# Eight scatter results over six PSUM banks: chunks 0, 1 and 4 in the banks of the up product and of the first result half

## The chip, the cores and the metric

One NeuronCore of a Trainium2 chip runs the whole program. The metric is the device time of one execution in microseconds; a kernel's time is the median of its runs. The trace comes from one profiled execution.

## The reference, cut to what matters

A decoder trunk of two layers over 512 tokens of width 1024, all float32. Each layer adds a mixer (a convolution block in layer 0, gated linear attention in layer 1), a cross-attention over 256 memory tokens, and a mixture of 32 experts of which each token uses 2. The change lies in the mixture of experts alone:

```python
def expert_block(args):
    xb, e = args
    return (jax.nn.silu(xb @ w_gate[e]) * (xb @ w_up[e])) @ w_down[e]

y_buf = lax.map(expert_block, (x_buf.reshape(n_blocks, MOE_BLOCK, D), block_expert)).reshape(-1, D)
y = y_buf[dest] * g_flat[order][:, None].astype(h.dtype)
out = jnp.zeros((T, D), h.dtype).at[token_idx].add(y)
```

Every expert has a 1024x512 gate matrix, a 1024x512 up matrix and a 512x1024 down matrix. Each expert's result rows are weighted and added to the rows of the tokens that chose it.

## The kernel before

**Tiling.** The residual stream xT is kept transposed: 8 chunks of 128 channels by 512 tokens. The experts are taken in 16 pairs per layer (`NP`), two experts with up to 64 tokens each side by side in the 128 columns of TensorE. A second, branched loop (`ROUNDS`) serves inputs where an expert has more than 64 tokens; it isn't entered with these inputs. Weights stream from HBM through a ring of six 2 MB slots, one for each of the six matrices of a pair; SyncE issues a load of 1 MB when TensorE has finished with the half slot that it overwrites (`pair_loads`, L990).

**One pair on TensorE**, in program order (`moe_segment` of the tensor block): `gates(p)` (L644), `up(p, 0)` which is the gate product into bank 0 (32 matmuls, L617), `scatter` of chunks 0 to 3 of the pair before, `up(p, 1)` into bank 1 (L617), `scatter` of chunks 4 to 7 of the pair before, `transposed(p)` into bank 4 (L662), a gather for the next pair-of-pairs (unit 9, L672; the last two pairs have none), `down(p)` into banks 2 and 3 (L632), another gather (unit 10), and `one_hot_T(p)` (unit 11, L681). After pair 15 one last `scatter(NP)` of all 8 chunks follows.

**Scatter** (L655) multiplies the pair's result by a one-hot matrix, two matmuls to a chunk (high part `yhi` with the chunk's first flag, low part `ylo`), each writing a full bank. VectorE adds each chunk to xT (`accumulate`, L1640). The operands `yhi` and `ylo` are copied out of banks 2 and 3 by ScalarE (L1255) and VectorE (L1666) in the pair before; `scatter` waits for `ylo_done`.

**Banks.** Banks 5, 6 and 7 are shared in rotation by everything that isn't a gate, up, down or transpose product. `unit(r, p, k)` numbers the uses: k=0 is the gates, k=1 to 8 the scatter chunks 0 to 7, k=9 and 10 the gathers, k=11 the one-hot transpose. Unit n uses bank 5 + n % 3, and TensorE first waits on `x_read` of that bank, which the reader of its last use raises. So chunk c + 3 waits until VectorE has added chunk c.

```python
                def use(p, k):
                    b, n = unit(r, p, k)
                    if not main or n:
                        pe.wait_ge(g[f"x_read{b}"], n)
                    return XBANK + b, g[f"x_full{b}"]
```

**One pair on VectorE**, in order: the next one-hot table (even pairs), `take_gates(p)`, `accumulate` of chunks 0 to 3, the product `hidden` from bank 1 (L1661), `accumulate` of chunks 4 to 7, `ylo` (L1666). ScalarE does the silu from bank 0 (L1248), `hidT` from bank 4 (L1250), the gathered tokens (L1238), `yhi` (L1255) and the one-hot transpose (L1260).

After the last pair of a layer ScalarE takes the chunks of xT as they are finished (`wait_x`), for the next norm.

Of the kernel before, what the change touches and what calls it, by code (L numbers as in the profile page):

```python
# [28 lines left out]
DEPTH = 2  # L29
# [21 lines left out]
RING = 6  # L51
HALF = C * 512 // 2
XBANK = 5
PER_ROUND = 64
HOTS = NQ + TT - 1
BANK = 512
BIG = 1.0e30
# [48 lines left out]
def build(nc, a, out):  # L106
# [13 lines left out]
    with ExitStack() as ctx:  # L120
# [110 lines left out]
        def bank(b, lo=0, hi=BANK):  # L231
# [61 lines left out]
        s_out = sem("s_out")  # L293
        SEG = ("gate_full", "up_full", "y_full", "silu_done", "gates_in", "gates_ready", "hidden_ready", "ht_full",
               "hidT_ready", "yhi_done", "ylo_done", "onehot_ready", "shifted",
               "x_full0", "x_full1", "x_full2", "x_read0", "x_read1", "x_read2")
        seg = [{x: sem(f"{x}_{l}") for x in SEG} for l in range(DEPTH)]
        ov_ld = [[[sem(f"ov_ld{l}_{i}_{h}") for h in range(2)] for i in range(RING)] for l in range(DEPTH)]

        def full(key):  # L300
            b, k = plan.at[key]
# [14 lines left out]
        def wait_x(eng, i, c):  # L316

            if i in (2, 3, 5, 6):
                eng.wait_ge(*read({2: ("co",), 3: ("xo", 0), 5: ("go",), 6: ("xo", 1)}[i] + (c,)))
            else:  # L320
                l = 0 if i == 4 else 1
                b, n = unit(0, NP, 1 + c)
                eng.wait_ge(seg[l][f"x_read{b}"], n + 1)

        def wait_h(eng, i, c):

# [5 lines left out]
        def unit(r, p, k):  # L332

            if p == -1:
                n = k - 8
            elif p == 0:
                n = 4 if k == 0 else k - 4
            elif p < NP - 2:  # L340
                n = 12 * p - 4 + k
            elif p == NP - 2:
                n = 12 * p - 4 + min(k, 9)
            else:
                n = 12 * p - 6 + min(k, 9) if p < NP else 12 * p - 9 + k
            return n % 3, PER_ROUND * r + n // 3

        def vector_rows(eng, names, done):
            for name in names:
# [24 lines left out]
        def _(pe):  # L374
# [214 lines left out]
            def moe_segment(l, r):  # L589
# [13 lines left out]
                def loaded(p, j, h):  # L603
                    n = moe_base[l] + j
                    if main:
                        pe.wait_ge(ring_ld[n % RING][h], 16 * ((n + RING * p) // RING + 1))
                    else:
                        pe.wait_ge(ov_ld[l][n % RING][h], 16 * (NP * r + p + 1 - NP))

                def up(p, kind, key):  # L610
                    x = xg[(p // 2) % 2]
                    for k in range(C):
                        if k % 4 == 0:
                            for e in range(2):
                                loaded(p, 2 * kind + e, k // 4)
                        for e in range(2):
                            mm = pe.matmul(PS[e * SL:(e + 1) * SL, kind * BANK:(kind + 1) * BANK],  # L617
                                           x[:, k, (2 * (p % 2) + e) * SL:(2 * (p % 2) + e + 1) * SL],
                                           ring[:, pair_slot(l, 2 * kind + e), k * 512:(k + 1) * 512],
                                           start=(k == 0), stop=(k == C - 1))  # L620
                        if k % 4 == 3:
                            mm.then_inc(g[key], 1)

                def down(p):
                    pe.wait_ge(g["hidT_ready"], NP * r + p + 1)
                    for k in range(FC):
                        if k % 2 == 0:
                            for e in range(2):
# [19 lines left out]
                def scatter(p, cs):  # L648
                    if cs[0] == 0:
                        pe.wait_ge(g["ylo_done"], NP * r + p)  # L650
                        taken(p - 1, 11)
                    for c in cs:
                        b, done = use(p, 1 + c)
                        for w in (yhi, ylo):
                            mm = pe.matmul(bank(b), w[:, c * P:(c + 1) * P], onehotT[:, :],  # L655
                                           start=(w is yhi), stop=(w is ylo))
                        mm.then_inc(done, 1)
# [110 lines left out]
            def moe(l):  # L768
# [20 lines left out]
                with pe.If(worst > SL):  # L789
                    with pe.Fori(1, ROUNDS) as r:  # L790
                        moe_segment(l, r)
                    for b in range(3):
                        pe.wait_ge(seg[l][f"x_read{b}"], PER_ROUND * ROUNDS)
                for b in range(3):
                    pe.wait_ge(seg[l][f"x_read{b}"], PER_ROUND)

            moe(0)

# [325 lines left out]
        def _(act):  # L1124
# [141 lines left out]
            def moe(l):  # L1266
# [5 lines left out]
                with act.If(worst > SL):  # L1272
                    with act.Fori(1, ROUNDS) as r:
                        moe_segment(l, r)
                    for b in range(3):
                        act.wait_ge(seg[l][f"x_read{b}"], PER_ROUND * ROUNDS)

            w = a["conv_w_dw"][0].rearrange("k (c p) -> (k c) p", p=P)
            for j in range(2):
# [148 lines left out]
        def _(dve):  # L1428
# [183 lines left out]
            def moe_segment(l, r):  # L1612
# [22 lines left out]

                def accumulate(p, cs):
                    for c in cs:
                        b, n = unit(r, p, 1 + c)
                        dve.wait_ge(g[f"x_full{b}"], n + 1)
                        dve.tensor_tensor(xT[:, c, :], bank(XBANK + b), xT[:, c, :], ALU.add).then_inc(g[f"x_read{b}"], 1)  # L1640

                if not main:
                    pf = ptab[:, :, :]
# [27 lines left out]
                accumulate(NP, range(0, C))  # L1671
                for b in range(3):
                    dve.wait_ge(g[f"x_read{b}"], PER_ROUND * r + PER_ROUND)
                return worst if main else None

            def moe(l):
# [246 lines left out]
```

## Time and profile before

| | |
|---|---|
| median of 3 runs | 1923.87 us (1920.25 to 1925.53) |
| the profiled execution | 1920.17 us |
| its span, first to last instruction | 1918.0 us |
| TensorE matmuls | 1864.5 us busy, 97% of the span |
| VectorE | 583.6 us, 30% |
| ScalarE | 373.6 us, 19% |
| GpSimd | 159.9 us, 8% |
| granted TensorE clock | 0.99 mean |

The 40 slices of the span, busy tenths (9 is 90% or more) and GB/s of the DMA engines:

```profile
PE   6999999998999999999999999999989999999997
DVE  3899221223122222222212322213222222222223
DMA  9214422102999999999861211302169999999992
GB/s 352 74 46 169 174 88 88 74 17 105 414 404 406 412 403 416 405 412 406 336 224 44 88 44 44 132 1 91 44 260 415 404 413 407 413 406 403 415 411 88
```

The two expert stages are the stretches where DMA stands at 9 and the rate at 403 to 416 GB/s, about 470 to 950 us and 1405 to 1895 us. A busy TensorE in these figures is one whose records follow each other; the end of a matmul is modelled, so short stalls between two matmuls don't lower the busy figure. They are seen in the distance from one start to the next.

### The profile page before, as it was taken

What the parts mean: (1) busy time and instruction counts of PE and PEld (TensorE: products, weight loads), DVE (VectorE), ACT (ScalarE), POOL (GpSimd) and SP (SyncE); (2) the same over time, 40 slices, a digit from 0 to 9 for tenths busy, and PEclk for the clock granted to TensorE, in tenths of its full rate; (3) what the DMA queues carried; (4) which work ended last, traced back from release to release, by engine and by line L of the source; (5) the groups of instructions that cost most, each with busy time, mean ns of one, the idle gap of its engine ahead of it and who ended that gap; (6) DMA issues with size and microseconds to landing.
All of it is one profiled execution on the core that took longest, in us unless ns stands there. A gap on an engine that the chain in (4) does not pass through costs nothing.

```text
span 1918.0 us, 18457 instructions
## 1 busy us (share of the span) xinstructions
PE 1864.5 (97%) x7584; PEld 924.7 (48%) x7584; DVE 583.6 (30%) x1104; ACT 373.6 (19%) x629; POOL 159.9 (8%) x151
## 2 busy tenths in 40 slices
PE   6999999998999999999999999999989999999997
PEld 5445644545445454444344444454454444445443
DVE  3899221223122222222212322213222222222223
ACT  2333211212111011111124232122111111111113
POOL 0466210010000000000020000100100000000001
PEclk9999999998999999999999999999989999999998
DMA  9214422102999999999861211302169999999992
GB/s 352 74 46 169 174 88 88 74 17 105 414 404 406 412 403 416 405 412 406 336 224 44 88 44 44 132 1 91 44 260 415 404 413 407 413 406 403 415 411 88
DMA packets 89869, 477.08 MB, mean 249 GB/s; under 512 B 7662, under 2 KB 8092, under 8 KB 40236
## 3 DMA queue, kind: packets, MB, share of 16 engines
q1 hardware_dynamic: 88636, 470.90, 61.2%
q0 software_dynamic: 592, 2.63, 0.5%
q10 hardware_dynamic: 544, 2.22, 0.3%
q8 instruction: 65, 1.06, 0.2%
q14 instruction: 32, 0.26, 0.0%
HBM read 471.53 MB, written 4.19 MB: 248 GB/s over the span
## 4 chain that ended last, share of the span: by engine, by line
PE 90%; DVE 7%; ACT 1%; issue 1%; DMA 0%; SPq 0%; DVEq 0%; ACTq 0%
PE PS L617 23%; PE PS L435 17%; PE PS L391 13%; PE PS L632 12%; PE PS L655 7%; PE PS L672 7%; DVE PS L1752 5%; PE PS L920 3%; PE PS L530 2%; PE PS L442 1%; PE PS L662 1%; PE PS L644 1%; PE PS L681 1%; DVE PS L1750 1%; PE PS L875 0%
## 5 line engine op out<-in xcount | busy, mean ns | idle before, releaser
L435 PE MATMUL PS<-hT,ring 128*128 128x512 f32 x640 | 279.4, 596 | 4.1 <-ACT hT L1149 3.4
L632 PE MATMUL PS<-ring,hT 128*64 128x512 f32 x1024 | 226.8, 595 | 2.7 <-ACT hT L1250 2.7
L617 PE MATMUL PS<-ring,hT 128*64 128x512 f32 x1024 | 226.3, 595 | 1.3 <-DVE small L1631 1.3
L617 PE MATMUL PS<-ring,xg 128*64 128x512 f32 x1024 | 226.8, 595 | 0.0
L1640 DVE TENSOR_TENSOR xT<-PS,xT 128x512 f32<-128x512 f32 x256 | 158.5, 681 | 211.6 <-PE PS L655 211.6
L435 PEld LDWEIGHTS PS<-hT,ring 128*128 128x128 f32 x640 | 121.4, 191 | 153.3 <-issue 152.4
L617 PEld LDWEIGHTS PS<-ring,hT 128*64 128x64 f32 x1024 | 73.9, 137 | 132.9 <-issue 131.2
L617 PEld LDWEIGHTS PS<-ring,xg 128*64 128x64 f32 x1024 | 72.4, 137 | 132.4 <-issue 132.2
L632 PEld LDWEIGHTS PS<-ring,hT 128*64 128x64 f32 x1024 | 70.7, 137 | 135.1 <-issue 127.9
L1666 DVE TENSOR_TENSOR ylo<-PS,yhi 128x1024 fp32r<-128x1024 f32 x32 | 39.2, 1224 | 301.7 <-ACT yhi L1255 301.7
L655 PE MATMUL PS<-onehotT,yhi 128*128 128x512 f32 x256 | 115.0, 449 | 3.6 <-DVE ylo L1666 3.6
L391 PE MATMUL PS<-ring,hT 128*128 128x512 f32 x256 | 111.8, 593 | 0.8 <-DVE RK L1793 0.8
L1752 DVE SCALAR_TENSOR_TENSOR PS<-RU,R,PS 128x512 f32<-128x512 f32 x168 | 111.3, 749 | 0.0
L655 PE MATMUL PS<-onehotT,ylo 128*128 128x512 f32 x256 | 101.1, 395 | 0.0
L1090 POOL TENSOR_TENSOR dg<-memT 128x512 f32<-128x512 f32 x6 | 7.6, 1272 | 1066.7 <-ACT memT L1144 1066.7
L1661 DVE SCALAR_TENSOR_TENSOR hT<-hT,small,PS 128x512 f32<-128x512 f32 x32 | 23.9, 747 | 212.5 <-PE PS L617 212.5
L1250 ACT ACTIVATE hT<-PS 128x512 f32<-128x512 f32 x32 | 19.1, 598 | 355.6 <-PE PS L662 355.6
L655 PEld LDWEIGHTS PS<-onehotT,yhi 128*128 128x128 f32 x256 | 47.8, 187 | 83.6 <-issue 48.7
L672 PE MATMUL PS<-onehot,hhi 128*128 128x256 f32 x512 | 88.1, 295 | 0.0
L435 PE MATMUL PS<-RC,ring 128*128 128x512 f32 x192 | 84.8, 594 | 0.0
L672 PE MATMUL PS<-onehot,hlo 128*128 128x256 f32 x512 | 82.8, 285 | 0.0
L672 PEld LDWEIGHTS PS<-onehot,hhi 128*128 128x128 f32 x512 | 71.1, 195 | 22.7 <-issue 22.7
(263 smaller groups left out, 1768.8 us busy)
## 6 DMA issues: line engine op xcount, KB each, us to landing
ring<-in_moe_w_gate SPq DMA_DIRECT2D x128, 1024.0 KB, 11.2
ring<-in_moe_w_up SPq DMA_DIRECT2D x128, 1024.0 KB, 12.1
ring<-in_moe_w_down SPq DMA_DIRECT2D x128, 1024.0 KB, 9.0
ring<-in_xa_w_kv SPq DMA_DIRECT2D x16, 1024.0 KB, 7.3
ring<-in_gla_w_in SPq DMA_DIRECT2D x12, 1024.0 KB, 12.8
ring<-in_conv_w_in SPq DMA_DIRECT2D x8, 1024.0 KB, 14.2
ring<-in_xa_w_q SPq DMA_DIRECT2D x8, 1024.0 KB, 6.8
ring<-in_xa_w_o SPq DMA_DIRECT2D x8, 1024.0 KB, 6.9
```

The lines of the kernel that those rows point to most:

```text
L391: mm = pe.matmul(o, lhs(k), rhs(k), start=(k == 0), stop=(k == nk - 1))
L435: mm = pe.matmul(bank(b), w[:, k * 512 + m * P:k * 512 + (m + 1) * P], src[:, k, :], start=(k == 0), stop=(k == C - 1))
L530: mm = pe.matmul(bank(b), w[:, k * 512 + m * P:k * 512 + (m + 1) * P], oT[:, k, :], start=(k == 0), stop=(k == C - 1))
L617: mm = pe.matmul(PS[e * SL:(e + 1) * SL, kind * BANK:(kind + 1) * BANK], x[:, k, (2 * (p % 2) + e) * SL:(2 * (p % 2) + e + 1) * SL], ring[ ...
L632: mm = pe.matmul(PS[e * SL:(e + 1) * SL, (2 + half) * BANK:(3 + half) * BANK], hidT[:, k, e * SL:(e + 1) * SL], ring[:, pair_slot(l, 4 + e ...
L655: mm = pe.matmul(bank(b), w[:, c * P:(c + 1) * P], onehotT[:, :], start=(w is yhi), stop=(w is ylo))
L672: mm = pe.matmul(bank(b, (c - c0) * 256, (c - c0 + 1) * 256), h[:, t, c * P:(c + 1) * P], onehot[:, q % 2, t, :], start=(h is hhi and t == 0),
L920: mm = pe.matmul(bank(b), w[:, k * 512 + (m % 4) * P:k * 512 + (m % 4 + 1) * P], goT[k], start=(k == 0), stop=(k == C - 1))
L1640: dve.tensor_tensor(xT[:, c, :], bank(XBANK + b), xT[:, c, :], ALU.add).then_inc(g[f"x_read{b}"], 1)
L1661: dve.scalar_tensor_tensor(hidden, sil, gcol, bank(1), ALU.mult, ALU.mult).then_inc(g["hidden_ready"], 1)
L1666: dve.tensor_tensor(ylo[:, :], PS[:, 2 * BANK:4 * BANK], yhi[:, :].bitcast(F32), ALU.subtract).then_inc(g["ylo_done"], 1)
L1752: ins = dve.scalar_tensor_tensor(acc, src, w, acc, ALU.mult, ALU.add)
```

## The change

The scatter's chunk 0 goes to bank 1 (where the up product lies) and chunks 1 and 4 to bank 2 (the first half of the down product). Chunks 2, 3, 5, 6 and 7 stay in the rotation of banks 5 to 7. Each of the two banks gets its own pair of semaphores, `z_full1`/`z_read1` and `z_full2`/`z_read2`. TensorE waits on `z_read1` before `up(p, 1)` and on `z_read2` before `down(p)`. The rotation has 9 units to a pair instead of 12 (7 for the last two pairs), 48 uses to a bank instead of 64. To make room for the new semaphores, the loads of the overflow loop, which isn't entered, share one semaphore per slot instead of two.

```diff
-PER_ROUND = 64
+PER_ROUND = 48
...
+               "z_full1", "z_read1", "z_full2", "z_read2")
...
-        ov_ld = [[[sem(f"ov_ld{l}_{i}_{h}") for h in range(2)] for i in range(RING)] for l in range(DEPTH)]
+        ov_ld = [[[sem(f"ov_ld{l}_{i}")] * 2 for i in range(RING)] for l in range(DEPTH)]
...
-                b, n = unit(0, NP, 1 + c)
-                eng.wait_ge(seg[l][f"x_read{b}"], n + 1)
+                _, _, done, n = result_bank(0, NP, c)
+                eng.wait_ge(seg[l][done], n + 1)
...
+            order = (0, 3, 4, 6, 7, 8, 9, 10, 11) if p < NP - 2 else (0, 3, 4, 6, 7, 8, 11)
             if p == -1:
                 n = k - 8
             elif p == 0:
-                n = 4 if k == 0 else k - 4
-            elif p < NP - 2:
-                n = 12 * p - 4 + k
-            elif p == NP - 2:
-                n = 12 * p - 4 + min(k, 9)
+                n = 4 + (0, 9, 10, 11).index(k)
+            elif p < NP:
+                n = 8 + 9 * min(p - 1, NP - 3) + 7 * max(p - NP + 2, 0) + order.index(k)
             else:
-                n = 12 * p - 6 + min(k, 9) if p < NP else 12 * p - 9 + k
+                n = 8 + 9 * (NP - 3) + 14 + order.index(k) - 1
             return n % 3, PER_ROUND * r + n // 3
+
+        def result_bank(r, p, c):
+            m = NP * r + (p - 1)
+            if c in (0, 1, 4):
+                b = 1 if c == 0 else 2
+                return b, f"z_full{b}", f"z_read{b}", m if c == 0 else 2 * NP * r + (2 * (p - 1) + c // 4)
+            b, n = unit(r, p, 1 + c)
+            return XBANK + b, f"x_full{b}", f"x_read{b}", n
...
                 def up(p, kind, key):
                     x = xg[(p // 2) % 2]
+                    if kind == 1 and (p or not main):
+                        pe.wait_ge(g["z_read1"], NP * r + p)
...
                 def down(p):
                     pe.wait_ge(g["hidT_ready"], NP * r + p + 1)
+                    if p or not main:
+                        pe.wait_ge(g["z_read2"], 2 * NP * r + 2 * p)
...
                     for c in cs:
-                        b, done = use(p, 1 + c)
+                        b, done, read_before, n = result_bank(r, p, c)
+                        if not main or n:
+                            pe.wait_ge(g[read_before], n)
+                        done = g[done]
                         for w in (yhi, ylo):
...
                 def accumulate(p, cs):
                     for c in cs:
-                        b, n = unit(r, p, 1 + c)
-                        dve.wait_ge(g[f"x_full{b}"], n + 1)
-                        dve.tensor_tensor(xT[:, c, :], bank(XBANK + b), xT[:, c, :], ALU.add).then_inc(g[f"x_read{b}"], 1)
+                        b, there, done, n = result_bank(r, p, c)
+                        dve.wait_ge(g[there], n + 1)
+                        dve.tensor_tensor(xT[:, c, :], bank(b), xT[:, c, :], ALU.add).then_inc(g[done], 1)
```

The waits at the end of a segment on TensorE, ScalarE and VectorE get the same two semaphores added.

## Rows read from the trace of the kernel before

**Rows 1.** Page: engines' busy time; then the chain that ended last, shares by engine.
```profile
PE 1864.5 (97%) x7584; PEld 924.7 (48%) x7584; DVE 583.6 (30%) x1104; ACT 373.6 (19%) x629; POOL 159.9 (8%) x151
PE 90%; DVE 7%; ACT 1%; issue 1%; DMA 0%; SPq 0%; DVEq 0%; ACTq 0%
```

**Rows 2.** Line L655: its counts, what ended idle time before it (us, times).
```profile
L655 PE MATMUL PS<-onehotT,yhi x256: 387/496/507, 506.7 to 1896.7; 128*128 128x512 f32 x128
...
  issue: 48.7, 60
  DVE xT L1640: 25.4, 70
  DVE ylo L1666: 7.4, 4
```

**Rows 3.** Chain in order of time, 700 to 735 us: start, us, what, count.
```profile
715.12 0.39 PE PS L644 x4
715.51 7.03 PE PS L617 x32
722.54 2.27 PE PS L655 x8
724.81 7.02 PE PS L617 x32
731.83 2.25 PE PS L655 x8
```

**Rows 4.** Timeline, scatter of chunks 0 to 3: start, us, instruction, [idle before].
```profile
722.81 0.39 PE L655 MATMUL PS<-onehotT,ylo 128*128 128x512 f32 x1
...
723.33 2.48 DVE L1640 TENSOR_TENSOR xT<-PS,xT 128x512 f32<-128x512 f32 x4 [6.63 <-PE PS L655]
...
723.73 0.40 PE L655 MATMUL PS<-onehotT,ylo 128*128 128x512 f32 x1
724.08 0.19 PEld L655 LDWEIGHTS PS<-onehotT,yhi 128*128 128x128 f32 x1 [0.39 <-DVE xT L1640]
...
724.41 0.40 PE L655 MATMUL PS<-onehotT,ylo 128*128 128x512 f32 x1
724.74 0.20 PEld L617 LDWEIGHTS PS<-ring,hT 128*64 128x64 f32 x4 [0.36 <-issue]
```

**Rows 5.** Timeline, scatter of chunks 4 to 7 and what follows.
```profile
731.95 0.75 DVE L1661 SCALAR_TENSOR_TENSOR hT<-hT,small,PS 128x512 f32<-128x512 f32 x1 [6.13 <-PE PS L617]
...
732.61 2.48 DVE L1640 TENSOR_TENSOR xT<-PS,xT 128x512 f32<-128x512 f32 x4
...
733.02 0.40 PE L655 MATMUL PS<-onehotT,ylo 128*128 128x512 f32 x1
733.35 0.19 PEld L655 LDWEIGHTS PS<-onehotT,yhi 128*128 128x128 f32 x1 [0.37 <-DVE xT L1640]
...
733.68 0.40 PE L655 MATMUL PS<-onehotT,ylo 128*128 128x512 f32 x1
...
734.26 0.55 PEld L672 LDWEIGHTS PS<-onehot,hhi 128*128 128x128 f32 x4
```

**Rows 6.** Timeline, last scatter of layer 1, all eight chunks.
```profile
1893.58 4.87 DVE L1640 TENSOR_TENSOR xT<-PS,xT 128x512 f32<-128x512 f32 x8 [0.82 <-PE PS L655]
...
1896.11 0.19 PEld L655 LDWEIGHTS PS<-onehotT,yhi 128*128 128x128 f32 x1 [0.30 <-DVE xT L1640]
...
1896.71 0.19 PEld L655 LDWEIGHTS PS<-onehotT,yhi 128*128 128x128 f32 x1 [0.30 <-DVE xT L1640]
```

**Rows 7.** Timeline, gates then gate product: an even pair, then an odd one.
```profile
714.96 0.56 PE L644 MATMUL PS<-gtab,onehot 128*128 128x6 f32 x4
715.45 1.08 PE L617 MATMUL PS<-ring,hT 128*64 128x512 f32 x4
...
745.77 0.56 PE L644 MATMUL PS<-gtab,onehot 128*128 128x6 f32 x4
746.26 1.51 PE L617 MATMUL PS<-ring,hT 128*64 128x512 f32 x6
```

**Rows 8.** Loads of up matrices in one pair: us of issue, first and last; to landing.
```profile
L990 SPq DMA_DIRECT2D ring<-in_moe_w_up x4: 327/380/433, 728.4 to 732.2; - x4
DMA to landing us min/median/max: 10.8/12.7/14.5
```

**Rows 9.** Stretches: us, PE PEld DVE ACT POOL busy, granted clock, DMA share, GB/s.
```profile
725.00:729.00 4.00, 4.00 (x20) 1.29 (x18) 0.82 (x2) 0.00 (x0) 0.00 (x0) 1.00 1.02 430
745.00:747.83 2.83, 2.83 (x21) 1.87 (x21) 1.17 (x4) 1.08 (x2) 0.00 (x0) 1.00 0.92 356
962.00:965.00 3.00, 0.15 (x1) 0.00 (x0) 1.15 (x2) 3.00 (x6) 2.71 (x3) 1.00 0.04 8
965.00:968.00 3.00, 2.50 (x5) 1.25 (x6) 0.06 (x1) 3.00 (x6) 2.71 (x3) 0.80 0.23 38
968.00:970.00 2.00, 2.00 (x3) 0.75 (x3) 0.00 (x0) 1.46 (x2) 1.71 (x3) 0.50 0.99 361
```

More of the change, by code:

```diff
@@ L295, in build @@
                "hidT_ready", "yhi_done", "ylo_done", "onehot_ready", "shifted",
-               "x_full0", "x_full1", "x_full2", "x_read0", "x_read1", "x_read2")
+               "x_full0", "x_full1", "x_full2", "x_read0", "x_read1", "x_read2",
+               "z_full1", "z_read1", "z_full2", "z_read2")
         seg = [{x: sem(f"{x}_{l}") for x in SEG} for l in range(DEPTH)]
-        ov_ld = [[[sem(f"ov_ld{l}_{i}_{h}") for h in range(2)] for i in range(RING)] for l in range(DEPTH)]
+        ov_ld = [[[sem(f"ov_ld{l}_{i}")] * 2 for i in range(RING)] for l in range(DEPTH)]
         def full(key):
@@ L607, in loaded @@
                     else:
-                        pe.wait_ge(ov_ld[l][n % RING][h], 16 * (NP * r + p + 1 - NP))
+                        pe.wait_ge(ov_ld[l][n % RING][h], 32 * (NP * r + p + 1 - NP))
                 def up(p, kind, key):
                     x = xg[(p // 2) % 2]
+                    if kind == 1 and (p or not main):
+                        pe.wait_ge(g["z_read1"], NP * r + p)
                     for k in range(C):
@@ L793, in moe @@
                         pe.wait_ge(seg[l][f"x_read{b}"], PER_ROUND * ROUNDS)
+                    pe.wait_ge(seg[l]["z_read1"], NP * ROUNDS)
+                    pe.wait_ge(seg[l]["z_read2"], 2 * NP * ROUNDS)
                 for b in range(3):
                     pe.wait_ge(seg[l][f"x_read{b}"], PER_ROUND)
+                pe.wait_ge(seg[l]["z_read1"], NP)
+                pe.wait_ge(seg[l]["z_read2"], 2 * NP)
             moe(0)
@@ L1276, in moe @@
                         act.wait_ge(seg[l][f"x_read{b}"], PER_ROUND * ROUNDS)
+                    act.wait_ge(seg[l]["z_read1"], NP * ROUNDS)
+                    act.wait_ge(seg[l]["z_read2"], 2 * NP * ROUNDS)
             w = a["conv_w_dw"][0].rearrange("k (c p) -> (k c) p", p=P)
@@ L1673, in moe_segment @@
                     dve.wait_ge(g[f"x_read{b}"], PER_ROUND * r + PER_ROUND)
+                dve.wait_ge(g["z_read1"], NP * r + NP)
+                dve.wait_ge(g["z_read2"], 2 * NP * r + 2 * NP)
                 return worst if main else None
```

## The prediction

> **What bounds the kernel now.** I read the page first. TensorE is busy 97% of the span and holds 90% of the chain that ended last; VectorE is busy 30%, and the chain has no share for DMA [rows 1]. So a change pays only if it shortens TensorE's own sequence, and it can do so only where TensorE stalls. Busy figures don't show short stalls, so the second view is line L655, the scatter, where the change acts. It has 256 chunks, 8 in each of 32 scatters (16 pairs, 2 layers). 70 of its weight loads were released by L1640, VectorE's add of an earlier chunk [rows 2]. That count can be taken apart: 30 scatters come in two groups of four chunks, and in each group only the fourth chunk meets a bank of the same group, which makes 60; the two scatters of eight at the end of a layer have five such chunks each, which makes 10. The rotation of three banks is thus what stalls it, once in every group of four.
>
> The third view is the timeline of one pair. In the first group the starts run at even distance while banks are free: 722.81 to 723.73 us is four intervals, 0.23 us each. Then chunk 3 starts 0.35 us after the matmul before it, and its second matmul 0.33 us later [rows 4]. The reason is seen beside it: VectorE started its four adds at 723.33, one lasts 2.48/4 = 0.62 us, and TensorE goes on 0.75 us after that start, once the first add is through. The second interval is long as well because the weight load that usually lies under the matmul before it is now exposed. The second group does the same: 0.33 and 0.33 us around chunk 7 [rows 5].
>
> **The change part by part.**
>
> *Chunk 3 and chunk 7 lose their wait.* The two long intervals fall back to 0.23 us. First group: 0.35 + 0.33 - 2 x 0.23 = 0.22 us. Second group: 0.33 + 0.33 - 0.46 = 0.20 us. Together 0.42 us a pair. That agrees with the chain, which has 2.27 and 2.25 us for eight matmuls [rows 3]. Pair 0 has no scatter, so it is 15 pairs in 2 layers: 30 x 0.42 = 12.6 us, all of it in TensorE's sequence.
>
> *Where the wait could go instead.* I followed each bank to its next user.
> - Chunk 0 now lies in bank 1, and `up(p, 1)` writes bank 1 right behind chunk 3. It waits for the add of chunk 0. That add is the one that releases chunk 3 today, at 724.08 us. Without the stall the up product would start at 724.74 - 0.22 = 724.52 us [rows 4]. Margin 0.44 us: hidden. If that cover were gone, every us of lateness would be paid 30 times, and behind it in TensorE's queue stand the up product, the second scatter group and all of the rest.
> - Chunks 1 and 4 lie in bank 2. Chunk 4 needs the add of chunk 1, which ended over 6 us before it. `down(p)` needs the add of chunk 4, which releases chunk 7 today at 733.35 us; the transposes and a gather lie between, and down starts after 734.26 us. Hidden.
> - Chunks 5, 6, 7 take the banks of the gates, chunk 2 and chunk 3, all read in the first half. Chunks 2 and 3 of a pair take the banks of gather 10 and of the one-hot transpose, both read by ScalarE in the pair before.
> - The gather behind the transposes takes chunk 5's bank, as it does now. Its first weight load is at 734.26 us, and would be at 734.06. The add of chunk 5 releases one add after that of chunk 4: 733.35 + 0.62 = 733.97 us [rows 5]. Margin 0.09 us, the thinnest. If it fails, the load is late by about 0.1 us. This gather exists in pairs 1 to 13, 26 times in all: bound 0 to 26 x 0.1 = 2.6 us. I take 0, since the row gives a margin, though a small one.
> - Banks 1 and 2 themselves must be free: bank 1 of the former up product, bank 2 of the former down result. The scatter already waits for `ylo_done`, which comes behind both readers on VectorE. No new wait.
>
> *Two more waits in each pair's TensorE queue* (`z_read1`, `z_read2`), both reached ahead of time. No row shows these two. The nearest is the step from the gates to the gate product: even pairs have up to four bank waits there that odd pairs lack, and both take 0.49 us from the first gate matmul to the first product [rows 7]. So a wait that is already met costs 0 there. As an upper bound I take the difference between two exits of the scatter: the step from the last scatter matmul to the up product is 724.74 - 724.41 = 0.33 us, against 0.23 between scatter matmuls. That is 0.10 us, wholly charged to waits: 60 x 0.10 = 6 us. A gain from one more wait is excluded, as it removes no work. I take 0, as the row at hand has four waits and no cost.
>
> *The last scatter of a layer.* VectorE's eight adds run without a gap, 4.87/8 = 0.61 us each, and TensorE's chunks come at the same pace, 1896.11 to 1896.71 = 0.60 us [rows 6]. VectorE sets it. With the change TensorE is done one chunk earlier, about 0.6 us, and what comes next waits for the adds. Gain 0; TensorE's idle time there grows by 0.6 us.
>
> *VectorE, ScalarE, the queues.* The adds keep their number, order and length; they read other banks. No DMA is moved or added. SyncE's loads are issued when TensorE finishes half slots, so they come 0.42 us earlier per pair. A pair moves 12 x 1.05 MB = 12.6 MB. While the queue is full the rate is 430 GB/s, and at the end of a period it dips to 356 [rows 9], so the backlog is cleared once a pair. At about 425 GB/s a pair needs 29.6 us; it has 30.8 now and would have 30.4. And were the loads to stay at today's pace, the lag would grow to 15 x 0.42 = 6.3 us, while the up loads land by 732.2 + 14.5 = 746.7 us [rows 8] and are first used one period after 724.74, at 755.6: 8.9 us of slack. DMA doesn't take the gain back either way. The overflow loop's semaphores cost nothing, since that loop isn't entered.
>
> **A rule that speaks against the change.** The granted clock is at 1.00 (2.4 GHz) when TensorE goes idle behind layer 0's last scatter (0.15 us busy from 962 to 965). It reads 0.80 from 965 to 968 and 0.50 (1.2 GHz) from 968 to 970, over the first projections of layer 1 [rows 9]. The change makes that idle time 0.6 us longer. The low stretch in these rows is 3 x 0.4 + 2 = 3.2 us of half clock and costs half of that, 1.6 us. Should it come out three times as long, that is 3.2 us more. The Trainium skill ("TensorE: Matmul & The Clock Gate", the table of why this matters for your kernels) advises against idle gaps of over about 3 us between bursts. By that rule the gap here is one already, and the rows agree: the clock does fall behind it. I keep the change of clock as a rival, not as a term.
>
> **The rivals.**
> 1. *Part of the stall comes back* at the thin margin of the gather, or as a price of the new waits: 12.6 - 2.6 = 10.0 at one end, 12.6 - 2.6 - 6 = 4.0 us at the other. Time 1913.9 to 1919.9. For it: 0.09 us of margin. Against it: [rows 7].
> 2. *The clock stays low for longer* behind layer 0: 12.6 - 3.2 = 9.4 us gained, 1914.5.
> 3. *The change doesn't do what it says.* The long intervals at chunks 3 and 7 would be a cost of the fourth chunk itself and stay: 1923.9. Against it: at a layer's end the same wait follows VectorE's pace to 0.01 us [rows 6], so it is the bank.
> 4. *Slower: the up product waits for VectorE.* The new wait on `z_read1` ties `up(p, 1)` to the add of chunk 0. If that add were released only with the fourth add of its group, it would be 3 x 0.62 = 1.86 us later, 1.42 past the margin. Net of the gain that is 1.0 us a pair, 30 us in all: 1953.9. It decides from 0.44 + 0.42 = 0.86 us of lateness on; below that the change still wins. Against it: VectorE had idled 6.63 us before these adds [rows 4], and each add signals by itself.
>
> **How the numbers follow.** Forecast, stall gone and nothing in its place: 0.70. Rival 1: 0.12. Rival 2: 0.08. Rival 3: 0.05. Rival 4: 0.05. The sum is made against the profiled execution, 1920.17 us (span 1918.0 and 2.2 around it): 1907.6 us. That execution lay 3.7 us under the median of the runs, at their lower edge; against the median it is 1923.87 - 12.6 = 1911.3 us, which I predict. The range: from the lowest run less the sum, 1920.25 - 12.6 = 1907.7, with 1 us for rounding in the intervals (0.42 is read to 0.01 on four of them): 1906.5. Upward, the highest run less the sum, 1912.9, plus 2.6 for the gather and 3.2 for the clock: 1918.5. About 0.3%, 5.8 us, is what can be told from no change. The forecast and rival 2 lie beyond that, and most of rival 1: faster 0.87. Rival 3 and the weak end of rival 1 give 0.08 for same, and slower 0.05.
>
> **What the new profile would show.** Right: the scatter's eight matmuls at 0.23 us each after the first, 2.05 us a group in place of 2.27 and 2.25; releases of L655 by L1640 down from 70 to those at the two layer ends; the period of a pair down from 30.8 to 30.4 us; L617 after the scatter still 0.33 us behind its last matmul. Wrong: a release of L617 by L1640 (rival 4), one of L672 by L1640 or longer steps before L617 and L632 (rival 1), a low clock beyond 970 us less the shift (rival 2), intervals over 0.3 us at chunks 3 and 7 (rival 3), or TensorE waiting for DMA late in a layer, which would void the slack that I counted.

## The result, and the profile after

| | before | changed |
|---|---|---|
| median, first measurement (4 and 4 runs) | 1922.06 us (1919.31 to 1925.53) | 1906.32 us (1905.97 to 1906.86) |
| ratio, 95% interval | | 0.9917 (0.9899 to 0.9936) |
| profiled execution, its span | 1920.17, 1918.0 | 1906.10, 1904.4 |
| mean granted clock in it | 0.990 | 0.991 |

The change saves 15.7 us in the medians, 0.8%, and 14.1 us between the two profiled executions. I had forecast 12.6 us and 1911.3, with a range down to 1906.5. The direction was right, and the measured time lies 0.2 us below the range. Two questions follow: was the sum of the stalls right, and where do the other microseconds come from?

In the changed kernel's lines the scatter is L672 (was L655), the gate and up products L629 (L617), the transposes L679 (L662), VectorE's add L1663 (L1640), and the first projection of layer 1 L445 (L435). First the chain in order of time, one pair, answering [rows 3]; columns are start, us, what, count.

```profile
691.72 2.07 PE PS L672 x8
693.79 7.02 PE PS L629 x32
700.81 2.05 PE PS L672 x8
702.85 0.47 PE PS L679 x4
```

A group of four chunks takes 2.07 and 2.05 us where it took 2.27 and 2.25. The timeline shows which intervals went, answering [rows 4]:

```profile
692.53 1.89 DVE L1663 TENSOR_TENSOR xT<-PS,xT 128x512 f32<-128x512 f32 x3 [7.37 <-PE PS L672]
...
692.94 0.39 PE L672 MATMUL PS<-onehotT,ylo 128*128 128x512 f32 x1
693.16 0.39 PE L672 MATMUL PS<-onehotT,yhi 128*128 128x512 f32 x1
693.39 0.40 PE L672 MATMUL PS<-onehotT,ylo 128*128 128x512 f32 x1
...
693.72 0.20 PEld L629 LDWEIGHTS PS<-ring,xg 128*64 128x64 f32 x4 [0.36 <-issue]
```

Chunk 3 starts at 693.16, 0.22 us behind the matmul before it, and its second part 0.23 us later: no wait and no exposed weight load. The up product still follows 0.33 us behind the last scatter matmul. And the releases of the scatter, answering [rows 2] (us, times):

```profile
  issue: 48.7, 60
  DVE ylo L1689: 7.4, 4
  DVE xT L1663: 0.4, 1
```

Of 70 releases by VectorE's add one is left, 0.4 us in all. The waits of the changed kernel name no release of L629, L646 or L689 by L1663, and none of these by a DMA.

To see where the rest comes from I cut each trace at the same four instructions: the first scatter matmul of layer 0, the first matmul of its last scatter, the same two of layer 1, and TensorE's last matmul. The numbers are differences of their start times. The table holds all four traces of each kernel; the later ones are from the experiments below.

| trace | up to the first scatter | stage, layer 0 | middle | half clock in the middle | stage, layer 1 | to the last matmul | end |
|---|---|---|---|---|---|---|---|
| before | 506.7 | 450.85 | 484.4 | 17.1 | 450.86 | 19.2 | 8.2 |
| before, 2nd | 508.1 | 450.89 | 482.2 | 13.7 | 450.86 | 19.2 | 8.2 |
| before, 3rd | 509.2 | 450.90 | 482.1 | 13.7 | 450.89 | 19.2 | 8.2 |
| before, 4th | 505.9 | 450.90 | 486.2 | 23.9 | 450.88 | 19.2 | 8.2 |
| changed | 509.3 | 444.31 | 481.8 | 13.7 | 444.31 | 19.2 | 7.2 |
| changed, 2nd | 506.7 | 444.30 | 480.5 | 10.2 | 444.31 | 19.2 | 7.2 |
| changed, 3rd | 508.3 | 444.27 | 481.9 | 13.7 | 444.27 | 19.2 | 7.2 |
| changed, 4th | 509.8 | 444.26 | 481.9 | 13.7 | 444.27 | 19.2 | 7.2 |

All are us. "Half clock" is the time in the middle part for which the trace grants 0.50. "End" runs from the last matmul's start to the end of the execution: 6.0 us within the span and 2.2 outside it in before, 5.5 and 1.7 in the changed kernel.

The stages repeat to 0.05 us. They fall by 6.6 us each, 13.2 us together, 0.44 us for each of 30 pairs. This is the scatter, and it is what the change does in every execution. The end is 1.0 us shorter in every trace; my sum had no term for it. The parts ahead of and between the stages vary by 3 to 4 us from one execution of a kernel to the next. In the middle the time follows the half clock, and where that is equal, 13.7 us, the two kernels differ by 0.3 us only. Ahead of the first scatter, the way from TensorE's 51st matmul to its 1201st, at about 430 us, repeats to 0.04 us in all eight traces; the spread lies in the first 28 us, where the granted clock first reaches 1.00 at 15.4 to 22.6 us, and behind 430 us, where half clock lasts 10.2 or 13.7 us.

### The profile page after: what moved, and what is told of

Read it like the earlier page. It is cut to its first block, busy times and chain, and to the rows that moved or that the text cites. A ratio compares the mean times of both kernels' runs of the same rounds, so it can differ in the third digit from the quotient of the medians.

```text
span 1904.4 us, 18491 instructions
## 1 busy us (share of the span) xinstructions
PE 1851.5 (97%) x7584; PEld 933.3 (49%) x7584; DVE 583.8 (31%) x1104; ACT 373.4 (20%) x629; POOL 159.8 (8%) x151
## 3 DMA queue, kind: packets, MB, share of 16 engines
q10 hardware_dynamic: 544, 2.22, 0.3%
## 4 chain that ended last, share of the span: by engine, by line
PE 90%; DVE 7%; ACT 1%; issue 1%; DMA 0%; SPq 0%; DVEq 0%; ACTq 0%
PE PS L629 24%; PE PS L445 17%; PE PS L401 13%; PE PS L646 12%; PE PS L689 7%; PE PS L672 7%; DVE PS L1777 5%; PE PS L941 3%; PE PS L540 1%; PE PS L452 1%; PE PS L679 1%; PE PS L658 1%; PE PS L698 1%; DVE PS L1775 1%; PE PS L896 0%
## 5 line engine op out<-in xcount | busy, mean ns | idle before, releaser
L445 PE MATMUL PS<-hT,ring 128*128 128x512 f32 x640 | 277.7, 593 | 3.7 <-ACT hT L1170 3.0
L646 PE MATMUL PS<-ring,hT 128*64 128x512 f32 x1024 | 226.8, 595 | 2.8 <-ACT hT L1271 2.8
L629 PE MATMUL PS<-ring,hT 128*64 128x512 f32 x1024 | 226.3, 595 | 1.3 <-DVE small L1654 1.3
L629 PE MATMUL PS<-ring,xg 128*64 128x512 f32 x1024 | 226.8, 595 | 0.0
L1663 DVE TENSOR_TENSOR xT<-PS,xT 128x512 f32<-128x512 f32 x256 | 158.7, 681 | 212.4 <-PE PS L672 212.4
L445 PEld LDWEIGHTS PS<-hT,ring 128*128 128x128 f32 x640 | 120.9, 190 | 151.7 <-issue 150.6
L629 PEld LDWEIGHTS PS<-ring,hT 128*64 128x64 f32 x1024 | 74.1, 137 | 132.7 <-issue 131.1
L629 PEld LDWEIGHTS PS<-ring,xg 128*64 128x64 f32 x1024 | 72.5, 137 | 132.2 <-issue 131.9
L646 PEld LDWEIGHTS PS<-ring,hT 128*64 128x64 f32 x1024 | 70.7, 137 | 135.1 <-issue 127.9
L672 PE MATMUL PS<-onehotT,yhi 128*128 128x512 f32 x256 | 108.2, 423 | 3.6 <-DVE ylo L1689 3.6
L672 PE MATMUL PS<-onehotT,ylo 128*128 128x512 f32 x256 | 101.9, 398 | 0.0
L689 PE MATMUL PS<-onehot,hhi 128*128 128x256 f32 x512 | 88.6, 297 | 0.0
L1684 DVE SCALAR_TENSOR_TENSOR hT<-hT,small,PS 128x512 f32<-128x512 f32 x32 | 23.9, 747 | 205.7 <-PE PS L629 205.7
L445 PE MATMUL PS<-RC,ring 128*128 128x512 f32 x192 | 84.8, 594 | 0.0
L689 PE MATMUL PS<-onehot,hlo 128*128 128x256 f32 x512 | 83.9, 287 | 0.0
L689 PEld LDWEIGHTS PS<-onehot,hhi 128*128 128x128 f32 x512 | 71.7, 196 | 22.7 <-issue 22.7
L672 PEld LDWEIGHTS PS<-onehotT,yhi 128*128 128x128 f32 x256 | 48.6, 190 | 61.5 <-issue 48.7
## 6 DMA issues: line engine op xcount, KB each, us to landing
ring<-in_conv_w_in SPq DMA_DIRECT2D x8, 1024.0 KB, 14.3
```

The lines of the kernel that those rows point to most:

```text
L445: mm = pe.matmul(bank(b), w[:, k * 512 + m * P:k * 512 + (m + 1) * P], src[:, k, :], start=(k == 0), stop=(k == C - 1))
L646: mm = pe.matmul(PS[e * SL:(e + 1) * SL, (2 + half) * BANK:(3 + half) * BANK], hidT[:, k, e * SL:(e + 1) * SL], ring[:, pair_slot(l, 4 + e ...
L689: mm = pe.matmul(bank(b, (c - c0) * 256, (c - c0 + 1) * 256), h[:, t, c * P:(c + 1) * P], onehot[:, q % 2, t, :], start=(h is hhi and t == 0),
L1663: dve.tensor_tensor(xT[:, c, :], bank(b), xT[:, c, :], ALU.add).then_inc(g[done], 1)
L1684: dve.scalar_tensor_tensor(hidden, sil, gcol, bank(1), ALU.mult, ALU.mult).then_inc(g["hidden_ready"], 1)
```

## The experiments

There are four groups of four runs. Each group was measured on a chip of its own beside the kernel before; its median there was 1919.91, 1920.91 and 1920.76 us (19, 23 and 15 runs) for the first three.

**The changed kernel again**, no edit.

> The changed kernel once more, to see how far its executions spread. The trace of the changed kernel gives 13.1 us less than that of before up to the last matmul: 2 x 6.5 us in the two expert stages (0.43 us in each of 30 pairs) and the rest from where stretches of half clock fall. Theory A (the scatter is worth 13 us, whatever is beyond it is where the half-clock stretches fall in an execution): the difference of medians lies anywhere from 11 to 17 us and changes from chip to chip, the pair's period is 30.4 us in every trace. Theory B (the change saves 15.7 us of itself): the difference of medians is 15.7 +- 1 us again, and a trace shows a further place of 2 to 3 us.

Median 1904.56 us (1899.64 to 1906.36, 6 runs), 15.4 us under before, ratio 0.9915 (0.9897 to 0.9933). The difference of medians is near the first one, as theory B wants; yet the trace has no further place of 2 to 3 us inside the stages, and its middle part alone is 4 us shorter than that of the first trace of before. Undecided by this run.

In the five runs on single banks the edit, against the changed kernel, is a table `MOVED` from chunk to bank. The rotation's numbers are then counted from a list of what is left in it, and a new wait whose bank isn't used falls away. Only the lines that differ from run to run are shown.

**Chunk 0 alone.**

```diff
+MOVED = {0: 1}
+TAIL = False
...
+LAST_MOVED = NP if TAIL else NP - 1
...
-            if c in (0, 1, 4):
-                b = 1 if c == 0 else 2
...
+            if c in MOVED and p <= LAST_MOVED:
+                b = MOVED[c]
```

> Only chunk 0 is moved, to bank 1; chunks 1 to 7 rotate over the three banks, the last scatter of a layer is as before. If each stall is its own bank wait: chunks 0 to 3 take 2.05 us and no longer 2.27, chunks 4 to 7 stay at 2.16 to their next instruction; 30 x 0.22 = 6.6 us below before, 1915.4. If the stall belonged to the fourth chunk as such, both stay, 1922.

Median 1914.32 us (8 runs), ratio 0.9964 (0.9950 to 0.9979), 5.6 us under before. From the chain in order of time of this kernel, first and second group:

```profile
719.78 2.04 PE PS L670 x8
728.83 2.26 PE PS L670 x8
```

The first group lost its stall, the second kept it. The stages are 447.5 us each, 3.4 less than before.

**Chunk 4 alone.**

```diff
+MOVED = {4: 2}
+TAIL = False
```

> Only chunk 4 is moved, to bank 2; the rest rotates, the last scatter is as before. By the bank theory the second group alone falls, from 2.16 to 1.96 us up to the transposes: 30 x 0.20 = 6.0 us below before, 1916. This and the run with chunk 0 alone should add up to the change, 12.6 us; by theory B something of 3 us is in neither of them.

Median 1915.93 us (12 runs), ratio 0.9972 (0.9959 to 0.9984), 4.0 us under before. Same view, first group and second group:

```profile
722.02 2.28 PE PS L670 x8
731.31 2.07 PE PS L670 x8
```

Now the second is free and the first is not. The stages are 447.9 us, 3.0 less. Each stall belongs to its own bank, and 3.4 + 3.0 = 6.4 us of the 6.6 us of a stage are in these two. The medians add up to 9.6 us only, where I had expected 12.6: the middle parts of these two traces are 487.7 and 485.3 us, longer than in all four and in three of the four traces of before, with 27.3 and 20.4 us of half clock. So the medians tell little about a few microseconds.

**Chunks 0 and 1 exchanged**: the up product waits for the second add.

```diff
+MOVED = {0: 2, 1: 1, 4: 2}
+TAIL = True
```

> As the changed kernel, but chunk 1 lies in bank 1 and chunk 0 in bank 2, so that the up product waits for the second add of VectorE, not the first. By my margin of 0.44 us against one add of 0.62 us the up product starts 0.18 us later in each of 30 pairs: 5.4 us slower than the changed kernel, 1911.7. If the margin is larger than an add, it equals the changed kernel, 1906.3; if a wait just missed costs an exposed weight load as well, up to 0.29 us a pair, 8.7 us slower.

Median 1911.53 us (6 runs; ratio to before 0.9953, 0.9936 to 0.9969), 7.0 over the changed kernel on the same chip. The first group with its way to the up product takes 2.22 us and not 2.05, 0.16 us more; the stages are 446.9 and 447.1 us, 5.4 us more together. The waits of this kernel have the 30 releases:

```profile
PEld PS L629 <- DVE xT L1663: 15.7, 30, 0.5
```

An add takes 0.61 us, so the margin is 0.61 - 0.16 = 0.45 us against the 0.44 that I had read.

**The new banks in the last scatter alone.**

```diff
+MOVED = {0: 1, 1: 2, 4: 2}
+TAIL = True
...
-            if c in (0, 1, 4):
-                b = 1 if c == 0 else 2
...
+            if c in MOVED and p == NP:
+                b = MOVED[c]
```

> The new banks in the last scatter of each layer alone; the 30 scatters inside the stages are as before. My working gave this part nothing. In the traces the start of the next layer's first projection comes 3.34 to 3.75 us behind TensorE's last scatter matmul in each kernel, and 0.6 to 0.7 us earlier against the start of the last scatter in the changed kernel without half clock. Theory C (TensorE's own way out of the stage runs from its last bank wait, so the earlier end of the scatter counts): from the start of layer 0's last scatter to the first projection 7.2 to 7.4 us in place of 8.0, and 0.6 us in the time, 1.0 at most. If VectorE's adds decide: 8.0 us, and the time of before.

Median 1919.26 us (12 runs), 1.7 us under before, ratio 0.9987 (0.9974 to 0.9999). The stages are 451.0 us each, unchanged to 0.2. The 1.7 us are more than the 1.0 that I had allowed, but not all of it is the way out of the layer: in the trace the end of the execution is 7.4 us in place of 8.2, and the projection comes at 8.45 us, with half clock over the scatter, where the three traces of before with half clock there have 8.80, 8.88 and 8.56. So something that I had put at nothing is worth 0.3 us there. The profile's chain names ScalarE as what the projection waits for, but ScalarE's steps don't line up with the projection's start: in before the sixth of its `hT` steps had ended 0.1 us ahead of it, in the changed kernel the fifth, 0.4 us ahead. What does line up is a row that the page doesn't count as busy, TensorE's branch around the overflow loop. One row each for before and for the changed kernel's second trace; durations in ns, then first and last start in us:

```profile
L789 PEldq COMPARE_BRANCH  x2: 3706/3782/3859, 961.4 to 1896.7; - x2
```

```profile
L806 PEldq COMPARE_BRANCH  x2: 3379/3388/3397, 954.3 to 1879.1; - x2
```

The last scatter started at 957.51 and 950.98 us. The branch starts 3.90 us after that in before and 3.31 us in the changed kernel, which fits the last bank wait, one add earlier; it takes 3.7 and 3.4 us; the projection starts 7.99 and 7.19 us behind the scatter's start. In this experiment, as in most traces, half clock lies over the last scatter (its 16 starts take 5.1 us in place of 3.8). With half clock there the projection starts at 8.80, 8.88 and 8.56 us in the other three traces of before, 8.75 in the mean, and at 8.50, 8.38 and 8.55 in those of the changed kernel, 8.48. The gain is thus 0.8 us between the two traces with full clock and 0.3 us in the mean with half. The branch's start moves by 0.6 us in both cases; the rest is the branch's own length, 3.4 to 3.9 us in the traces of either kernel, and a step of 0.4 to 0.6 us from its end to the projection. In layer 1 the way out gains nothing: TensorE's next matmul starts 10.9 us behind the last scatter's start in all eight traces.

**Fillers that keep the clock up**, in the kernel before and in the changed one: matmuls into a bank that nobody reads then.

```diff
+                if main:
+                    busy(0, 6)
                 scatter(NP, range(0, C))
+                if main:
+                    busy(0, (12, 26)[l])
...
                 b = take(("cs", l))
+                busy(b, 14)
```

> The kernel before with matmuls that nobody reads in three idle places of TensorE (14 ahead of the router's sums, 6 ahead of the last scatter, 12 and 26 behind it), to keep the clock up there. Theory A (the rest beyond 13.1 us is the clock): fewer stretches of half clock in the trace, and the middle stage, from layer 0's last scatter to layer 1's first, shorter than the 484.4 us of before, toward 479 to 481; runs lie closer together than the 10 us of before. If the fillers stand in the way instead of filling, the middle stage grows by up to 3 us.

> The same fillers in the changed kernel. Theory A: with the clock alike on both sides the difference to the kernel before with fillers is the scatter alone, 13.1 us and up to 0.7 for the way out of layer 0, so 13 to 14 us. Theory B: 15 to 16 us again.

Medians 1921.05 us (12 runs; ratio to before 0.9995) and 1906.80 us (6 runs; 0.9919, 0.9903 to 0.9935), granted clock 0.995 and 0.995 where it was 0.990. Their difference is 14.3 us: 0.3 above the 13 to 14 of theory A and below the 15 to 16 of theory B. The stages differ by 13.3 us. As a remedy the fillers fail: the branch behind them starts at 5.17 and 4.74 us in place of 3.90 and 3.31, and the projection at 9.27 and 8.70 us in place of 7.99 to 8.88 and 7.19 to 8.55, so what the clock gives back is paid there. My expectation for the middle, 479 to 481 us, was missed: 482.1 and 483.5, the latter with a stretch of half clock at 1310 us. The runs of before with fillers lie within 6.2 us of each other, those without on the same chip within 9.7.

**Chunk 3 in bank 1**: the mechanism of my slower rival, made on purpose.

```diff
+MOVED = {0: 2, 3: 1, 4: 2}
+TAIL = True
```

> As the changed kernel, but chunk 3 lies in bank 1 and chunks 0 and 4 in bank 2, so the up product right behind chunk 3 waits for the fourth add: the mechanism of my slower rival, made on purpose. By the rival's price the add comes 3 x 0.62 = 1.86 us later than that of chunk 0, 1.42 past the margin of 0.44: 30 x 1.42 = 42.6 us over the changed kernel, some 1948, and 28 over before. If the margin or the adds are other than I read them, the price per pair shows it, 1.2 to 1.6 us.

Median 1947.60 us (4 runs), ratio to before 1.0135 (1.0114 to 1.0156), 26.7 us over before on the same chip, where the price said 28. The changed kernel was not measured on this chip; against its median on the chip of the first group it is 43.0 us, against that of the first measurement 41.3, where the price said 42.6. Its waits show the wait that replaced the stall:

```profile
PE PS L629 <- DVE xT L1663: 38.7, 30, 1.3
```

A pair's first group takes 3.41 us against 2.05: 1.36 us, 30 times; the stages are 41.0 us longer together. Three adds of 0.61 less 1.36 give a margin of 0.47 us. Rival 4 is real; the change escapes it by which chunk it puts there.

**Without the overflow loop and its branch**, before and changed. These two leave out a part that these inputs don't enter.

```diff
-                with pe.If(worst > SL):
-                    with pe.Fori(1, ROUNDS) as r:
-                        moe_segment(l, r)
...
```

> The kernel before without the overflow loop and its branch on every engine (a part left out that these inputs don't enter). TensorE's branch behind the last scatter takes 3.4 to 3.9 us in the traces and starts when the last bank wait is passed. Theory C (the branch decides when layer 1's first projection starts): it starts when VectorE's adds are done, some 5.9 us behind the start of the last scatter in place of 8.0, and the time is 1.5 to 2.2 us under before. If ScalarE decides, as the chain of waits names it, the start stays at 8.0.

> The changed kernel without the overflow loop and its branch. By theory C the scatter's earlier end is worth nothing here: also 5.9 us from the last scatter's start to the projection, and the two kernels without the branch differ by the stages alone, 13.1 us, and by what the clock adds. Against the changed kernel it gains 1.3 us. If the 0.8 us were of another kind, the two would still differ by it, 13.9 us in the traces with the clock taken out.

Medians 1917.87 us (11 runs), ratio 0.9982 (0.9973 to 0.9992), and 1903.98 us (5 runs). In before the loop and its branch together are worth 2.9 us, more than the 1.5 to 2.2 that I had expected; in the changed kernel 0.5 us against its 1904.46 below, less than the 1.3. The traces say why: without the loop the end of the execution is 6.9 us in both kernels, 1.3 under before and 0.3 under the changed kernel, and this trace of the changed kernel has a stretch of half clock at 1306 to 1309 us that takes back what the way out gave. The projection's start is now released by VectorE's add. From the timeline of before without the branch:

```profile
961.35 3.15 DVE L1623 TENSOR_TENSOR xT<-PS,xT 128x512 f32<-128x512 f32 x5 [0.16 <-PE PS L655]
...
964.71 1.53 PE L435 MATMUL PS<-hT,ring 128*128 128x512 f32 x3 [1.21 <-DVE xT L1623]
```

It comes 6.88 us behind the scatter's start here and 6.87 us in the changed kernel without the branch, both with half clock over the scatter; the 5.9 that I expected was worked out for full clock. So the branch decides, not ScalarE, and without it the scatter's earlier end is worth nothing. The pair differs by 13.9 us in the medians and by 13.3 us in the stages: with the way out and the end alike, little more than the scatter is left.

**Eight banks for the last scatter.**

```diff
+                to = 0 if (p, c) == (NP, 4) else b
...
+            to = {6: 3, 7: 4}[c] if p == NP and c > 5 else XBANK + b
...
-                        if not main or n:
+                        if (not main or n) and not (p == NP and c in (4, 6, 7)):
```

> The changed kernel, with chunks 4, 6 and 7 of the last scatter of each layer in banks 0, 3 and 4, which nobody needs by then: eight banks, no wait in it. By theory C the branch starts 1.6 us earlier than in the changed kernel, at 1.7 us behind the scatter's start in place of 3.3, it ends before VectorE's adds do, and the first projection of layer 1 starts at 5.9 to 6.2 us in place of 7.2: 1.0 to 1.3 us under the changed kernel. If the branch is not what decides, nothing changes.

> The changed kernel again on the same chip, as the measure for the three others. 7.2 us from layer 0's last scatter to the projection where the clock is up; 444.3 us in each stage between the first and the last scatter; 14 to 15 us under before in the medians.

Medians 1906.81 us (5 runs; ratio to before 0.9921, 0.9904 to 0.9938) and, for the changed kernel, 1904.46 us (5 runs; 0.9908, 0.9892 to 0.9925), 16.3 us under before where I had expected 14 to 15; its stages are 444.3 us as expected. The mechanism works: in layer 0 the branch starts 0.06 us behind the scatter's start (I had said 1.7, but with no wait in the way the sequencer goes past the scatter's sixteen matmuls at once), and the projection starts at 6.87 us in place of 8.38.

```profile
PE PS L447 <- DVE xT L1665: 1.3, 1, 1.3
```

Yet the time is 2.4 us longer, not 1.0 to 1.3 shorter. By its trace 1.7 us of that lie ahead of the first scatter (510.0 against 508.3), and the 1.5 us at the exit are offset by half clock at 1310 us, in the same middle part. The mean clock was 0.988 to 0.989 in its runs against 0.990 to 0.991. It is no better kernel as measured. Why its executions run at a lower clock isn't known.

**Further traces of both kernels**, no edit, on a fourth chip.

> The kernel before, a further trace. If its half-clock stretches fall on costlier places in general: middle part 484 us or more as in the first trace, against 480.5, 481.8 and 481.9 in the three traces of the changed kernel, of which 0.8 is TensorE's way out. If the first trace was a chance: 481.8 to 482.7 in most traces, and the rest of the difference lies ahead of layer 0's first scatter or isn't there.

> The kernel before, a further trace: middle part 484 us if the costly places of the half clock are the rule, 481.8 to 482.7 if they are chance.

> The kernel before, a third further trace: middle part 484 us if the costly places of the half clock are the rule, 481.8 to 482.7 if they are chance.

> The changed kernel, a further trace on the same chip: middle part 480.5 to 481.9 us, stages 444.3 us each; the time up to layer 0's first scatter anywhere from 505.5 to 509.2 us, as in all kernels so far.

Single times 1919.36, 1920.49, 1921.23 and 1906.65 us. The middle parts stand in the table above: 482.2, 482.1 and 486.2 us, and 481.9. The changed kernel's first scatter comes at 509.8 us, past the 505.5 to 509.2 that I had given. Neither the rule nor the chance that I had set against each other holds cleanly: two of four traces of before are costly, none of four of the changed kernel. What is costly is seen in the clock. Stretches of the last trace of before, then of the changed kernel's second trace (columns as in [rows 9]):

```profile
957.00:961.00 4.00, 4.00 (x12) 3.12 (x12) 2.94 (x5) 2.74 (x5) 0.29 (x1) 0.57 0.00 0
961.00:964.00 3.00, 1.30 (x6) 0.65 (x4) 2.31 (x4) 3.00 (x7) 2.71 (x3) 1.00 0.02 5
964.00:971.00 7.00, 5.68 (x7) 2.52 (x8) 0.06 (x1) 4.73 (x8) 6.27 (x7) 0.52 0.52 165
1315.80:1319.30 3.50, 3.50 (x5) 1.44 (x6) 0.08 (x1) 0.14 (x1) 0.00 (x0) 0.52 0.47 197
```

```profile
951.00:955.00 4.00, 4.00 (x16) 2.83 (x16) 3.25 (x6) 2.52 (x5) 0.06 (x1) 1.00 0.00 0
958.00:965.00 7.00, 6.83 (x16) 3.15 (x17) 0.06 (x1) 4.95 (x8) 6.27 (x6) 1.00 0.43 138
1306.00:1310.00 4.00, 4.00 (x10) 1.71 (x9) 0.00 (x0) 0.00 (x0) 0.00 (x0) 1.00 0.37 158
```

In 7 us that begin idle (1.3 and 0.2 us of them) and go over into the projections, TensorE starts 7 matmuls at 0.52 and 16 at 1.00. The half clock before them, from 957 to 961, follows an idle stretch of 1.8 us in which TensorE waits for `ylo`; the one from 964 on follows the idle time up to the projection. Compared matmul by matmul, the costliest middle (486.2) falls behind the cheapest (480.5) at the last scatter, at the first projections and at 1317 to 1319 us, by over 5 us of the 5.7 together: at these stretches and the way out.

The other executions have no trace, but each has its mean granted clock. Of the 58 executions of before measured beside the four groups, 16 have 0.986 or 0.987 and take 1922.3 to 1926.8 us, and 40 have 0.990 or 0.991 and take 1916.5 to 1921.7. Of 16 executions of the changed kernel none is below 0.988. Yet this is not what makes the difference of the medians: among executions at 0.990 and 0.991 alone the medians differ by 15.0 us on the first group's chip and by 16.0 on the third's.

## Why the prediction missed, point by point

**Held.** What bounds the kernel, and that busy figures hide the stalls. The count of 60 stalled chunks in 30 scatters and of 10 in the last two: one release of 70 is left. That each stall is the bank's and not the fourth chunk's: the two single moves take one each. That nothing takes its place: no release of the up product by an add, of the gather behind the transposes, or by a DMA. The thinnest margin, 0.09 us, was enough. The margin of 0.44 us before the up product: 0.45 and 0.47 in the two kernels that use it up, and the price of crossing it (rival 4) came out at 41.0 for 42.6 us in the stages. The two new waits cost nothing: with them the first group takes the 2.05 us that I had worked out. VectorE sets the pace of the adds in the last scatter.

**The term of the stalls, slightly small.** 0.42 us a pair, read from four intervals of one pair to 0.01 us each; measured 0.44. In the means over the 30 pairs the way from the scatter's first matmul to the next product falls from 2.280 to 2.054 us and the second from 2.164 to 1.953. That is 13.1 and not 12.6 us, and 13.2 by the stages as a whole. A mean over many pairs would have had it.

**The way out of the layer: the step that failed.** I wrote "what comes next waits for the adds. Gain 0". It doesn't. The projection waits for TensorE's own branch, 3.4 to 3.9 us long, which starts behind the last bank wait, and that wait comes one add earlier. The gain is 0.8 us in the traces with full clock, 0.3 with half clock over the scatter. For the same reason rival 2 was built on a wrong sign: TensorE's idle time behind the last scatter did not grow by 0.6 us. From the last scatter matmul to the projection it went from 3.75 to 3.34 us. The Trainium skill ("TensorE: Matmul & The Clock Gate", the table of why this matters for your kernels) warns of gaps of over about 3 us. Here the clock also fell to half behind the gap of 1.8 us ahead of layer 0's last scatter, in six of eight traces, so the traces don't agree with that figure as a bound. But the same gap of 1.8 us stands ahead of layer 1's last scatter, and there it fell in none of the eight: the gap's length alone doesn't decide.

**The end of the program, a term that was left out.** I wrote "The overflow loop's semaphores cost nothing, since that loop isn't entered" and gave the end of the execution no term. It is 1.0 us shorter in every trace of the changed kernel, 7.2 for 8.2 us; the 2.2 us outside the span, which my sum took over from before, are 1.7 in all its runs. It isn't the moved banks inside the stages: the run that moves them in the last scatter alone has an end of 7.4 us, that with chunk 4 alone 7.3. All of these share the loop's semaphores as the changed kernel does, and without the loop the end is 6.9 us with and without the change. That points at the overflow loop as it was built, but no run changes its semaphores alone, so the cause stays open.

**The base, the largest single part of the miss.** I took the sum off the median of three runs, 1923.87 us, although I noted that the profiled execution lay 3.7 us lower. With a fourth run that median is 1922.06, and over 15 to 23 runs it is 1919.9 to 1920.9. My second number, 1920.17 - 12.6 = 1907.6 us for the profiled execution, missed its counterpart by 1.5 us; the one for the median missed by 5.0: 1.8 of it from the base within the first measurement, 0.6 from the stalls, 1.0 from the end, 0.3 to 0.8 from the way out, and some 1 us from the clock and chance.

**The range.** Its lower end was the lowest of three runs less the sum, with 1 us for rounding. All unknowns were added upward, to the gather and to a clock that stays low longer. Executions of one kernel differ by 3 us before the first scatter and by up to 4 us in the middle, and that can fall either way. The term left out at the lower end was the clock.

**What stays open.** 13.2 us are in the stages, 1.0 us at the end and 0.3 to 0.8 us at the way out, 14.5 to 15.0 together. The medians differ by 15.4 to 16.3 us. The four profiled executions of each kernel differ by 15.3 us in the mean, and the parts add up to it: 13.2 in the stages, 1.0 at the end, 2.2 in the middle (483.7 to 481.5), the way out included, less 1.1 by which the time up to the first scatter rises (507.4 to 508.5). That the scatter's 13.2 us are of the change is shown. Whether the change makes the costly half-clock stretches rarer (two of four traces against none of four, and 16 of 58 executions at the lowest clock against none of 16), or whether this and about 1 us are chance, is not settled. The new banks don't rule such stretches out: the one at about 1310 us stands in the traces of three other kernels that have them (with fillers, without the branch, with eight banks).

## What to carry to other kernels

Where a rotation of buffers is one short of a burst, the stall is paid in every burst and hardly shows in busy time; look at the distance between starts, and count its releases against the loop's structure. A result may borrow the bank of a product whose next writer is far away; what matters is the first reader's place in the order, since the add of the first chunk comes 0.45 us in time, that of the second 0.16 us late and that of the fourth 1.36 us late. And before a few microseconds are forecast off a median, see how far it lies from the profiled execution, and let the clock's spread widen the range on both sides. A code path that isn't entered can still cost time, in the branch around it and, as these runs suggest, at the program's end.

## What the runs showed of the hardware

A branch of TensorE's queue around a loop that isn't entered takes 3.3 to 3.9 us, and here it hid only where the sequencer got to it early: with no bank wait ahead of it, it starts 0.06 us behind the first of sixteen matmuls; with the waits of before, 3.90 us.

The granted clock falls to 0.50 (1.2 GHz) also within 0.8 us of the end of a gap of 1.8 us without matmuls, at the start of layer 0's last scatter, in 6 of the 8 traces of the two kernels; behind the same gap in layer 1 it does so in none. It falls at other places in other executions of the same program. In the middle part of the kernel before, with 13.7 to 23.9 us of half clock, this made 4 us between its four traces.
